# Five of the last eight modulations between the chunks of the first query product

## What is computed

```python
sh1, sc1, g1, sh2, sc2, g2 = jnp.split(mod.astype(x.dtype), 6, axis=-1)
...
x = x + g1 * m
h = rmsnorm(x, norm2_g) * (1 + sc2) + sh2
x = x + g2 * peer(h, peer_wq, peer_keys, peer_u, peer_v)
```

## Time and profile before

| | us |
|---|---|
| median of 3 runs | 2081.55 (2080.81 to 2082.29) |
| the profiled execution: time | 2080.06 |
| its span | 2078.2 |
| TensorE busy in the span | 2013.0 (97%) |
| VectorE busy | 1559.3 (75%) |
| GpSimdE busy | 926.1 (45%) |
| ScalarE busy | 912.4 (44%) |
| mean granted clock of TensorE, of full speed | 0.987 |

### The profile page before, as it was taken

How to read it: one execution, slowest core, us unless ns; L and a number is a source line. 1 busy time by engine, 2 the same in 40 slices (tenths; PEclk the granted TensorE clock), 3 DMA queues, 4 the chain that set the end, 5 groups by cost and what they waited for, 6 DMA issues and landing times.

```text
span 2078.2 us, 34663 instructions
## 1 busy us (share of the span) xinstructions
PE 2013.0 (97%) x11788; PEld 1872.0 (90%) x11788; DVE 1559.3 (75%) x2872; ACT 912.4 (44%) x1508; POOL 926.1 (45%) x652
## 2 busy tenths in 40 slices
PE   4999998999899999999999999999999999999997
PEld 3999998999799999999899999999999999999987
DVE  5559998352479999995666666657888888888887
ACT  3445554222432323233688888863333233332322
POOL 1233332333133477777765666664333333333352
PEclk9999999999899999999999999999999999999997
DMA  9212122434522488888888888779999999999993
GB/s 384 107 61 67 62 60 74 177 122 168 198 62 65 142 302 304 301 306 301 279 333 316 320 330 318 287 251 366 350 346 349 349 344 398 348 344 349 348 361 120
DMA packets 172454, 523.05 MB, mean 252 GB/s; under 512 B 17616, under 2 KB 71248, under 8 KB 170704
## 3 DMA queue, kind: packets, MB, share of 16 engines
q1 hardware_dynamic: 97776, 267.67, 36.7%
q0 software_dynamic: 55296, 201.35, 27.1%
q10 hardware_dynamic: 19296, 52.96, 6.4%
HBM read 463.71 MB, written 58.20 MB: 251 GB/s over the span
## 4 chain that ended last, share of the span: by engine, by line
PE 87%; DMA 5%; DVE 3%; ACT 2%; issue 2%; POOL 1%; SPq 0%; ACTq 0%; DVEq 0%; POOLq 0%
PE P L847 28%; PE P L757 28%; PE P L570 22%; PE P L781 4%; DMA gel_scratch<-gel 2%; PE P L658 1%; DMA rows<-in_v_tab,Eg 1%; PE P L602 1%; PE P L721 1%; DMA tb<-in_posT 1%; DMA raw<-in_wblk 1%; ACT hs L871 1%; ACT hHi L871 1%; PE P L611 0%; PE P L813 0%
## 5 line engine op out<-in xcount | busy, mean ns | idle before, releaser
L871 ACT ACTIVATE wHi<-raw 128x1024 fp32r<-128x1024 f32 x330 | 346.3, 1049 | 1028.7 <-PE P L847 419.0
L512 POOL DMA_INDIRECT rows<-in_v_tab,Eg x192 | 223.6, 1164 | 379.8 <-DVE accB L1711 222.6
L495 POOL TENSOR_TENSOR wLo<-raw,wHi 128x1024 fp32r<-128x1024 f32 x128 | 308.8, 2412 | 182.3 <-ACT wHi L871 179.6
L757 PE MATMUL P<-hHi,wHi 128*128 128x448 f32 x1024 | 380.3, 371 | 3.0 <-POOL wLo L495 3.0
L489 POOL TENSOR_TENSOR wLo<-raw,wHi 128x1024 fp32r<-128x1024 f32 (+1 forms) x76 | 186.1, 2450 | 438.1 <-ACT wHi L871 431.2
L757 PE MATMUL P<-hLo,wHi 128*128 128x448 f32 x1024 | 376.9, 368 | 0.0
L757 PE MATMUL P<-hHi,wLo 128*128 128x448 f32 x1024 | 376.7, 368 | 0.0
L570 PE MATMUL P<-hHi,wHi 128*128 128x320 f32 x960 | 230.1, 321 | 20.2 <-DVE hLo L1300 10.6
L1675 DVE TENSOR_TENSOR pairs<-P,keysel 128x1024 f32<-128x1024 f32 x112 | 132.1, 1220 | 130.4 <-PE P L781 128.1
L570 PE MATMUL P<-hLo,wHi 128*128 128x320 f32 x960 | 221.1, 311 | 0.0
L570 PE MATMUL P<-hHi,wLo 128*128 128x320 f32 x960 | 220.9, 311 | 0.0
(11 more groups left out here) (243 smaller groups left out, 3820.0 us busy)
## 6 DMA issues: line engine op xcount, KB each, us to landing
raw<-in_ublk SPq DMA_DIRECT2D x128, 512.0 KB
raw<-in_v_tab SPq DMA_DIRECT2D x128, 512.0 KB
raw<-in_wblk SPq DMA_DIRECT2D x104, 512.0 KB
gel_scratch<-gel ACTq DMA_DIRECT2D x128, 224.0 KB
gsr<-gel_scratch SPq DMA_DIRECT2D x128, 224.0 KB
gate_scratch<-stage ACTq DMA_DIRECT2D x5, 4096.0 KB, 15.2
gates4a<-gate_scratch SPq DMA_DIRECT2D x16, 640.0 KB
gates4b<-gate_scratch SPq DMA_DIRECT2D x16, 640.0 KB
```

The lines of the kernel that those rows point to most:

```text
L495: pool.tensor_tensor(wLo[:, n % 2, :], raw[:, n % 4, :], wHi[:, n % 2, :].bitcast(f32), ALU.subtract).then_inc(raw_used[n % 4], 1)
L512: pool.indirect_dma_start(out=row(n), out_offset=None, in_=tab, in_offset=bass.IndirectOffsetOnAxis(ap=Eg[:, buf, at:at + 1], axis=0)).the ...
L757: last = nc.tensor.matmul(P[0][:, h, 0:TD], w_[:, h, k * 128:(k + 1) * 128], x_[:, k, C0:T], start=(k == 0 and a == 0 and b == 0), stop=(k ...
L871: return nc.scalar.activation(out, in_, f, **kw)
```

## The change

Modulations 43 to 47 are taken out of the sequence ahead of `wq 0`. `product` gets a parameter `between`, a function that is called after each chunk. For `wq 0` it is `last_modulations`: after chunk 0 comes modulation 43; after chunk n (1 to 4) the turn of modulation 42 + n and then modulation 43 + n; after chunk 5 the turn of 47. ScalarE copies rows 41 and 42 ahead of the norm's chunks, and row 43 + k behind hHi of chunk k, for k = 0 to 4. Nothing is added to the work or taken from it, and SyncE's and VectorE's programs stay as they are.

```diff
-        def product(name, m, hi, lo, kk=KC, settled=None):
+        def product(name, m, hi, lo, kk=KC, settled=None, between=None):
...
                                                     stop=(k == kk - 1 and a == 1))
+                if between is not None:
+                    between(k)
             last.then_inc(s["prod_done"], 1)
...
         modulation_turn(40)
-        modulation_parts(41)
-        for m in range(42, 48):
-            modulation_turn(m - 1)
+        for m in range(41, 43):
             modulation_parts(m)
-        modulation_turn(47)
+            modulation_turn(m)
         pe.wait_ge(s["keys_ld"], 16)
+
+        def last_modulations(n):
+
+            if 1 <= n <= 5:
+                modulation_turn(42 + n)
+            if n < 5:
+                modulation_parts(43 + n)
...
-        product("wq", 0, hHi, hLo, settled=S_H2)
+        product("wq", 0, hHi, hLo, settled=S_H2, between=last_modulations)
...
-            for m in range(41, 46) if n else range(14, 16):
+            for m in range(41, 43) if n else range(14, 16):
                 mod_row(m)
...
                 actf(hHi[:, k, :], hs[:, k, :], ACT.Copy).then_inc(s["hi_ready"], 1)
-                if n and k < 2:
-                    mod_row(46 + k)
+                if n and k < 5:
+                    mod_row(43 + k)
```

## The result

| | before | changed |
|---|---|---|
| median, us | 2081.18 (2080.01 to 2082.29, 4 runs) | 2102.89 (2101.53 to 2105.13, 4 runs) |
| the profiled execution, us | 2080.06 | 2101.53 |
| its span, us | 2078.2 | 2099.7 |
| TensorE busy in the span, us | 2013.0 | 2019.0 |
| mean granted clock, of full speed | 0.987 | 0.980 |

The changed kernel is slower by 1.06% (ratio 1.0106, 95% interval 1.0090 to 1.0122), 21.7 us between the medians. The forecast was 2101.8 us, in a range from 2095 to 2105.

The account below looks back on a forecast made before the run. TensorE, busy 97% of the span, bounds the kernel. Start 5.08 us earlier, five turns of 31.4 us, then chunks 5 to 7 end wq 0 20.2 us later; added to the median 2081.55: 2101.8 us, range 2095 to 2105.

Parts of the forecast that it names:

- The earlier start: Chunk 0 of wq 0 on TensorE starts at 538.49 against 543.57, 5.08 us earlier, read from the first norm.
- The ring: ScalarE, VectorE and TensorE wait in a circle, one chunk at a time: five turns, 31.4 us; at 1.2 GHz, 74%.
- From the end of hHi to TensorE's start: Hand-over from ScalarE's scaled chunk to TensorE's matmuls, taken as 1.01 us in each turn.
- from turn to row: On TensorE, a turn and the next modulation up to the start of ScalarE's row: 1.64 us.
- The price for going from the chunk's weights to the modulation's and back: TensorE's switch between 128-column and 32-column weights: taken as zero, 0.3 us a turn allowed, 1.5 in all.
- The clock: TensorE's granted clock was to be 0.50 from 536 to 574 us or so, through the ring.
- Rival 1: TensorE's clock stays at or returns to 2.4 GHz in the ring: 11.9 us later, 2093.5 to 2098 us; 19%.
- Small matmuls: By the skill page a modulation takes an estimated 0.5 us, loss 17 us; the forecast kept the measured 1.08 us.
- Rival 2: ScalarE's rows are ready in time, so no ring closes: wq 0 ends 2.3 us earlier, 2079.2 us; 3%.
- the price of a row: ScalarE's copy of one modulation's row between chunks, 0.27 us for each of five.
- Rival 3: Part of the loss is taken back behind wq 0, at most 7.6 us of TensorE's idle time; 2094 to 2098; 3%.
- The sum: All terms up to the end of wq 0: 575.1 against 554.93, 20.2 us later, passed on to the end.

Follow-up runs that it names:

- e4_ring_fill: Changed kernel plus unread matmuls in TensorE's idle time, 36 ahead of wq 0, 16 behind each of modulations 43 to 47; reciprocal to transposes 36.91 us, +12.62 against before.
- e6_lag2_fill: e3_lag2 plus 29 unread matmuls on TensorE ahead of wq 0; reciprocal to transposes 21.42 us, -2.87 against before; whole-time ratio 0.9989.
- e3_lag2: Changed kernel with ScalarE's row 43+k two chunks later, behind hHi of chunk k+2; reciprocal to transposes 22.93 us, -1.36 against before; ratio 1.0005.
- e2_lag1: Changed kernel with ScalarE's row 43+k one chunk later, behind hHi of chunk k+1; reciprocal to transposes 25.56 us, +1.27 against before; ratio 1.0015.
- e1_rows_only: Kernel before with only ScalarE's new row order, all modulations still ahead of wq 0; reciprocal to transposes 24.63 us, +0.34; ratio 1.0004.
- e5_before_fill: Kernel before plus unread matmuls in TensorE's waits, 6 ahead of modulation 43, 3 behind each of 43 to 47; reciprocal to transposes 26.65 us, +2.36; ratio 0.9997.

## Why the prediction held, step by step

- **The earlier start.** Forecast 538.49, measured 539.79 in an execution whose reciprocal began 1.31 us later (531.95 against 530.64). By the stretch, 7.85 was forecast (538.49 - 530.64) and 7.84 measured. The first norm was the right row to read it from.
- **The ring.** Forecast 31.4 us from chunk 0 to chunk 5, measured 30.5 (539.79 to 570.29), in turns of 6.06, 5.91, 6.31, 5.92 and 6.30 where 6.04, 6.15, 6.53, 6.15 and 6.53 were forecast. Two terms were a little too big. From the end of hHi to TensorE's start 1.01 us was taken for all chunks; only the first has it (538.79 to 539.79), the others 0.90 (550.86 to 551.76). And from turn to row 1.64 us was read behind a wait of TensorE; behind a chunk it is 1.50 (547.61 to 549.11). The price for going from the chunk's weights to the modulation's and back, for which 0.3 us a turn were allowed, is nearly nothing: 0.12 us in the first turn (539.79 to 541.66 is 1.87 against 1.75).
- **The clock.** At 1.2 GHz through the ring and back at 574 to 576, as forecast. Rival 1 (the clock stays up) didn't occur, and e4_ring_fill gave its price: 11.7 us where 11.9 had been worked out. The page "TensorE: Matmul & The Clock Gate" of the Trainium skill, under "A second HAM failure mode", has a clock that goes back and forth when short waits stand between groups of matmuls; here it was 0.50 without a break from 536 to 574 us.
- **Small matmuls.** By Part 3 (Packing small matmuls) of the same page of the Trainium skill a modulation would take an estimated 0.5 us at 1.2 GHz. The trace has 1.08 us again, in the ring as before it, so the measured row was the one to go by.
- **Rival 2, the open ring.** Worked out at -2.3 us; e6_lag2_fill, which opens it and has the full clock, measured -2.87, and e3_lag2 -1.36 with the first microseconds at half clock. Most of the 0.6 us between -2.3 and -2.87 is the price of a row: 0.27 us were taken for each of the five, and a row that waits for nothing takes 0.16 (543.63 to 543.79 in e6_lag2_fill). The theory of the ring stands on these two, e2_lag1 and the changed kernel, which all have TensorE's order in common (but for the filling), and on e1_rows_only, which has ScalarE's new order without the ring.
- **Rival 3, part taken back.** Not seen: the time from the transposes to the end is 1524.1 us against 1523.3.
- **The sum.** The stretch grew by 19.3 us (forecast 20.2), the span by 21.5. Of the other 2.2 us, 1.3 lie ahead of the stretch and 0.9 behind it, where the two programs are the same; the first product of the first norm is already 0.74 us later (52.49 against 51.75). That is the scatter of executions. That the median fell within 1.1 us of the forecast is therefore partly luck: terms too big by 0.9 us in all and a scatter of 2, where other runs of the kernel before have medians 2.0 and 4.7 us above the 2081.18 of these.

## What to carry to other kernels

When a step is moved next to the work that it should hide behind, follow its wait around: an engine that works its list in order turns "wait for the other engine's last step" into a ring as soon as that step stands behind something which this engine has yet to feed. The length of one turn is the sum of all work and hand-overs in it, and it replaces the slowest engine's pace. The cure is distance, not order: in the stretch, the same rows one chunk later cost 1.3 us and two chunks later nothing (-1.4), where at distance zero they cost 19.3. In whole times even the open ring is not clear of the kernel before, so no gain from the move could be measured here.

## What had not been expected of the hardware

In e5_before_fill TensorE was busy 2.00 of 2.00 us in every stretch from 534 to 550 us (two are shown) and the granted clock stayed at 0.50, with modulations (32-column weights) for 1.01 of every 2.33 us (540.35 to 541.36) ahead of wq 0; in e4_ring_fill, matmuls of 320 columns alone brought it from 0.50 at 536 to 1.00 at 540. A busy TensorE in the profile does not promise the higher clock; which property of the work decides was not separated. And of the change's 19.3 us some 7.6 were the clock: a turn of the ring takes 5.9 to 6.3 us at 0.50 and, with the idle time filled, 4.6 to 5.0 us at 1.00.
